# Merge stage of a hybrid-attention step: norm, residual and split of h by runs of 384 columns, gate blocks 0 and 1 by runs between embedding pieces

## The chip, the cores and the metric

One core of one Trainium2 chip. The metric is the device time in microseconds of one execution of the whole program. Several executions are timed and their median is given; one more is recorded by the hardware profiler, and everything said of engines comes from that one.

## The reference, cut to what matters

```python
def merge(oa, za, ob, zb, w_out):
    return jnp.concatenate([oa * jax.nn.silu(za), ob * jax.nn.silu(zb)], axis=-1) @ w_out

def finish(x, mix, p, post_g, w_gate, w_ple, ple_g):
    h = x + rms_norm(mix, post_g)
    return h + jax.nn.sigmoid(h @ w_gate) * rms_norm(p @ w_ple, ple_g)
```

There are 1152 tokens (1024 of a prompt and 8 x 16 of samples) and 1024 features; `w_out` and `w_gate` are 1024 x 1024, `p` has 256 features. Everything ahead of this (the input projection and two attentions) is not touched.

## The kernel before, in words

The program runs in stages, and the last one is the function `merge` (L1508). All data lie feature-major: a block of 128 features is on the 128 partitions, and the 1152 tokens run along the free dimension. A product writes PSUM in three runs of 384 tokens, one bank each (`RUN`, `NCH`); `acc[0]` and `acc[1]` are two sets of three banks, and `small` is two banks more.

A product in near-float32 is three passes (L231): the weight and the data are each split into a high part (`w_hi`, `a_hi`) and a low part (`w_lo`, `a_lo`), and high x high, high x low and low x high are added up. One output block of 128 features over 8 blocks of input features and 3 runs is 72 matmuls of 384 columns. A weight block is loaded by SP's queue (L1575 to L1606) into one of two `w_raw` slots, its high part is made by ScalarE (`high`, L1613), its low part by GpSimd (`low`, L1691).

The stage has these steps:

- Eight blocks of the output projection (`multiply(0)` to `multiply(7)`, L1767). VectorE copies each into `mix` (L1841), ScalarE squares it (L1623), VectorE adds the squares (L1826).
- The embedding p @ w_ple, eight blocks of six plain float32 matmuls (`embed`, L1740; each shows as two records in the trace). Their weights share the two `w_raw` slots with the gate weights. The first two blocks are held in `work` until `mix` has been read.
- Between them: 9 small matmuls sum the squares over the partitions (`statistics(0)`, L1747), VectorE and ScalarE make the reciprocal root, VectorE spreads it over diagonals (L1832), and three matmuls bring it to all partitions (`to_all(0)`, L1756). VectorE copies the three runs into `rms` (L1836).
- h, block by block of 1152 columns: VectorE scales `mix` (L1847); the residual is added into `x` by VectorE for blocks 0 and 2 (L1852) and by GpSimd for the others (L1702); ScalarE moves or takes an embedding block into `mix` (L1653, L1656) and makes the high part of h (L1663); VectorE makes the low part (`low`, L1795), three blocks behind.
- Eight gate blocks h @ w_gate (`multiply(GATE0)` and on, L1777 to L1789). Inside block 1 stands `statistics(1)` and inside block 2 `to_all(1)`, for the norm of the embedding; ScalarE squares all eight embedding blocks (L1623 again) for it. ScalarE takes the sigmoid of each block (L1681), and VectorE finishes the output (L1862, L1869, L1871).

Each engine runs its own list of instructions in the order written, and waits on semaphores. A gate block i of 2 or more writes the banks of block i - 2, and so waits for that block's sigmoid. What GpSimd's queue holds around h is: residual adds 1, 3, 4, 5, the low part of gate weight 0, adds 6 and 7, the low part of gate weight 1.

```python
multiply(GATE0, (h_hi_done, h_lo_done))
multiply(GATE0 + 1, between={5: lambda: statistics(1)})
multiply(GATE0 + 2, between={2: lambda: to_all(1)})
```

Of the kernel before, what the change touches and what calls it, by code (L numbers as in the profile page):

```python
# [243 lines left out]
def run(x, n):  # L244
    return x[:, n * RUN:(n + 1) * RUN]
# [1262 lines left out]
def merge(nc, w_slot, z_sample, xT, pT, w_out, w_gate, w_ple, yT, qo, ident, ones, g_sub, g_post, g_ple):  # L1508
# [5 lines left out]
    PLE0, GATE0, END = NB, 2 * NB, 3 * NB  # L1514
    with ExitStack() as ctx:
# [5 lines left out]
        w_raw, w_hi, w_lo = weight_slots(mk, w_slot)  # L1521
        work = [mk.sb(f"work{s}", [P, TOK]) for s in range(2)]
# [26 lines left out]
        def split_count(j):  # L1549


            return j if j < PLE0 else j - GATE0 + NB

        def loads_of_slot(j):

            here = j // 2 + 1 if j < PLE0 else NB // 2 + 1 + (j >= GATE0) * ((j - GATE0) // 2 + 1)
            return here - (j % 2 == 0 if j < PLE0 or j >= GATE0 else j < PLE0 + NB // 2)

        BY_DVE = (0, 2)

        def wait_h(eng, j):
            if j in BY_DVE:
                eng.wait_ge(h_by_dve, 1 + BY_DVE.index(j))
            else:
                eng.wait_ge(h_by_pool, sum(i not in BY_DVE for i in range(j + 1)))

        def ple_weights(j):

            return w_raw[j // 4][:].rearrange("p (b k) c -> p b k c", k=PKT)[:, j % 4]
# [4 lines left out]
        def _(sp):  # L1574
            sp.dma_start(w_raw[1][:], w_out[1]).then_inc(w_in[1], 16)  # L1575
            for j in range(2, 4):
                if j > 2:
                    sp.wait_ge(w_lo_done, split_count(j - 2))
                sp.dma_start(w_raw[j % 2][:], w_out[j]).then_inc(w_in[j % 2], 16)
# [4 lines left out]
            for j in range(4, NB):  # L1584
                sp.wait_ge(w_lo_done, split_count(j - 2))
                sp.dma_start(w_raw[j % 2][:], w_out[j]).then_inc(w_in[j % 2], 16)
            for r in range(2):
                sp.wait_ge(w_lo_done, split_count(NB - 2 + r))
                sp.dma_start(w_raw[r][:].rearrange("p (b k) c -> p b (k c)", k=PKT),
                             w_ple[4 * r:4 * r + 4].rearrange("b p k c -> p b (k c)")).then_inc(w_in[r], 16)  # L1590
            for r in range(2):
                sp.wait_ge(product, PLE0 + 4 * r + 4)
                sp.dma_start(w_raw[r][:], w_gate[r]).then_inc(w_in[r], 16)
# [5 lines left out]
            for j in range(2, NB):  # L1599
                sp.wait_ge(w_lo_done, split_count(GATE0 + j - 2))  # L1600
                sp.dma_start(w_raw[j % 2][:], w_gate[j]).then_inc(w_in[j % 2], 16)
                if j >= 4:
                    store_y(j - 4)
# [8 lines left out]
        def _(act):  # L1612
            def high(j):  # L1613
                act.wait_ge(w_in[j % 2], 16 * loads_of_slot(j))
                if j >= 2:
                    act.wait_ge(product, j - 1 if j < PLE0 or j >= GATE0 + 2 else NB)
                act.activation(w_hi[j % 2][:], w_raw[j % 2][:], ACT.Copy).then_inc(w_hi_done, 1)
# [21 lines left out]
            for j in range(NB - 2, NB):  # L1639
                act.wait_ge(mix_out, j + 1)  # L1640
                square(j, 0)
            for j in range(2):
                act.wait_ge(product, PLE0 + j + 1)
                act.wait_ge(added, NB - 1 + j)
                act.activation(by_runs(work[j][:]), acc[j][:, :, 0:RUN], ACT.Copy).then_inc(ple_out, 1)
                if j == 0:
                    mix_norm.scalar(act)

            def take_ple(j):
                wait_h(act, j)  # L1650
                if j < 2:
                    act.wait_ge(ple_out, 2)
                    act.activation(mix[:, j, :], work[j][:], ACT.Copy).then_inc(ple_moved, 1)  # L1653
                else:
                    act.wait_ge(product, PLE0 + j + 1)
                    act.activation(by_runs(mix[:, j, :]), acc[j % 2][:, :, 0:RUN], ACT.Copy).then_inc(ple_out, 1)  # L1656

            for j in range(NB):
                if j == 1:
                    take_ple(2)  # L1660
                if j != 2:
                    take_ple(j)
                act.activation(a_hi[:, j, :], x[:, j, :], ACT.Copy).then_inc(h_hi_done, 1)  # L1663
                if j == NB // 2:
                    high(GATE0)
            high(GATE0 + 1)
            act.wait_ge(ple_out, NB)
            act.wait_ge(ple_moved, 2)
            for j in range(NB):
                square(j, NB)  # L1670
            ple_norm.scalar(act)

            for j in range(GATE0, END):
                i = j - GATE0
                act.wait_ge(product, j + 1)
                if i < 2:
                    act.wait_ge(added, 2 * NB)
                else:
                    act.wait_ge(ple_gated, i - 1)
                if j < END - 1:  # L1680
                    act.activation(by_runs(work[j % 2][:]), acc[j % 2][:, :, 0:RUN], ACT.Sigmoid).then_inc(sigmoid, 1)  # L1681
                else:
                    for n in range(NCH):
                        act.wait_ge(product, j + 1 + n)
                        act.activation(run(work[j % 2][:], n), acc[j % 2][:, n, 0:RUN], ACT.Sigmoid).then_inc(sigmoid, 1)
                if j + 2 < END:
                    high(j + 2)

        @block.gpsimd
        def _(pool):  # L1690
            def low(j):  # L1691
                pool.wait_ge(w_hi_done, split_count(j))
                pool.tensor_tensor(w_lo[j % 2][:], w_raw[j % 2][:], w_hi[j % 2][:].bitcast(F32),  # L1693
                                   ALU.subtract).then_inc(w_lo_done, 1)

            for j in range(1, NB):
                low(j)
            pool.wait_ge(x_in, 16 * KT)
            for j in range(1, NB):
                if j not in BY_DVE:  # L1700
                    pool.wait_ge(normed, j + 1)
                    pool.tensor_tensor(x[:, j, :], x[:, j, :], mix[:, j, :], ALU.add).then_inc(h_by_pool, 1)  # L1702
                if j == NB // 2 + 1:
                    low(GATE0)
            for j in range(GATE0 + 1, END):
                low(j)

        @block.tensor
        def _(pe):
            def free_banks(j):  # L1710

                if j >= GATE0 + 2:
                    pe.wait_ge(sigmoid, j - GATE0 - 1)
                elif j >= PLE0 + 2:
                    pe.wait_ge(ple_out, j - PLE0 - 1)
                elif j >= 2:
                    pe.wait_ge(mix_out, j - 1)

            def multiply(j, parts=(), between={}):
                if j > 0:  # L1720
                    pe.wait_ge(w_lo_done, split_count(j))
                free_banks(j)
                for k in range(KT):
# [4 lines left out]
                    for n in range(NCH):  # L1728
                        last = three_passes(pe, acc[j % 2][:, n, 0:RUN], w_hi[j % 2][:, k, :], w_lo[j % 2][:, k, :],
                                            run(a_hi[:, k, :], n), run(a_lo[:, k, :], n),  # L1730
                                            start=(k == 0), stop=(k == KT - 1))
                last.then_inc(product, 1)

            def embed(j):
                i = j - PLE0
                pe.wait_ge(w_in[i // 4], 16 * loads_of_slot(j))
                free_banks(j)
                for k in range(PKT):
                    for n in range(NCH):
                        last = pe.matmul(acc[j % 2][:, n, 0:RUN], ple_weights(i)[:, k, :], run(p_emb[:, k, :], n),  # L1740
                                         start=(k == 0), stop=(k == PKT - 1))
                last.then_inc(product, 1)
# [27 lines left out]
            pe.wait_ge(p_in, 16)  # L1770
            embed(PLE0)
            statistics(0)
            embed(PLE0 + 1)
            to_all(0)
            for j in range(PLE0 + 2, GATE0):
                embed(j)
            multiply(GATE0, (h_hi_done, h_lo_done))  # L1777
            multiply(GATE0 + 1, between={5: lambda: statistics(1)})
            multiply(GATE0 + 2, between={2: lambda: to_all(1)})
            for j in range(GATE0 + 3, END - 1):  # L1780
                multiply(j)
            pe.wait_ge(w_lo_done, split_count(END - 1))
# [9 lines left out]
        def _(dve):  # L1792
# [35 lines left out]
            def spread_norm(norm, which):  # L1828
# [5 lines left out]
                for n in range(NCH):  # L1834
                    dve.wait_ge(spread, NCH * which + n + 1)
# [138 lines left out]
```

## Time and profile before

| | |
|---|---|
| median of 3 runs | 870.44 us (870.25 to 870.54) |
| the profiled execution's own time | 871.64 us |
| its span in the trace | 869.8 us |
| mean granted TensorE clock over the span | 0.973 |
| TensorE matmul busy | 799.1 us, 92% of the span |
| VectorE / ScalarE / GpSimd busy | 412.9 / 332.7 / 192.9 us |
| DMA, mean over the span | 106 GB/s |

Times in rows count from the start of the span. A row of an instruction runs from its start to its acknowledged end, so the next one on the same engine can start some 0.1 us before the row ends; the distance from start to start is what an instruction costs in a full queue. A row that was made to wait inside the engine is longer by that wait. An engine's idle time before a row stands in brackets with what ended it. The merge stage takes the last 265 us.

### The profile page before, as it was taken

What the parts mean: (1) busy time and instruction counts of PE and PEld (TensorE: products, weight loads), DVE (VectorE), ACT (ScalarE), POOL (GpSimd) and SP (SyncE); (2) the same over time, 40 slices, a digit from 0 to 9 for tenths busy, and PEclk for the clock granted to TensorE, in tenths of its full rate; (3) what the DMA queues carried; (4) which work ended last, traced back from release to release, by engine and by line L of the source; (5) the groups of instructions that cost most, each with busy time, mean ns of one, the idle gap of its engine ahead of it and who ended that gap; (6) DMA issues with size and microseconds to landing.
All of it is one profiled execution on the core that took longest, in us unless ns stands there. A gap on an engine that the chain in (4) does not pass through costs nothing. (4 is left out here: it accounts for less than half of the span.)

```text
span 869.8 us, 13090 instructions
## 1 busy us (share of the span) xinstructions
PE 799.1 (92%) x5207; PEld 714.3 (82%) x5207; DVE 412.9 (47%) x947; ACT 332.7 (38%) x679; POOL 192.9 (22%) x165
## 2 busy tenths in 40 slices
PE   5999999999978989697769999997999998899998
PEld 6999999999965657564458999897999984498998
DVE  6743231011039889587572222232613438966553
ACT  7321011100016788597574444345411213452111
POOL 0122122122111000153433333222211203812220
PEclk9999999999999999889899999998899999899999
DMA  8142343212011000390026666761611100102301
GB/s 327 48 179 113 103 157 106 76 49 82 0 29 45 1 1 2 98 382 22 1 98 225 241 237 233 269 226 49 270 75 49 49 0 25 49 25 90 117 33 78
DMA packets 35993, 92.58 MB, mean 106 GB/s; under 512 B 4696, under 2 KB 13912, under 8 KB 33752
## 3 DMA queue, kind: packets, MB, share of 16 engines
q1 hardware_dynamic: 33488, 82.23, 26.7%
q10 hardware_dynamic: 2448, 9.57, 2.9%
q8 instruction: 38, 0.62, 0.3%
q14 instruction: 19, 0.16, 0.1%
HBM read 76.13 MB, written 16.58 MB: 107 GB/s over the span
## 5 line engine op out<-in xcount | busy, mean ns | idle before, releaser
L233 PE MATMUL in_acc<-in_x_hi,w_hi 128*128 128x384 f32 x216 | 74.6, 346 | 9.4 <-DVE in_x_lo L427 8.7
L234 PE MATMUL in_acc<-in_x_lo,w_hi 128*128 128x384 f32 x216 | 74.1, 343 | 0.0
L235 PE MATMUL in_acc<-in_x_hi,w_lo 128*128 128x384 f32 x216 | 74.0, 343 | 0.0
L233 PE MATMUL in_acc<-in_x_hi,in_w_hi 128*128 128x384 f32 x216 | 72.7, 336 | 0.0
L233 PE MATMUL mrg_acc<-mrg_a_hi,w_hi 128*128 128x384 f32 x192 | 67.0, 349 | 6.1 <-issue 3.0
L235 PE MATMUL in_acc<-in_x_hi,in_w_lo 128*128 128x384 f32 x216 | 72.2, 334 | 0.0
L234 PE MATMUL in_acc<-in_x_lo,in_w_hi 128*128 128x384 f32 x216 | 72.2, 334 | 0.0
L234 PE MATMUL mrg_acc<-mrg_a_lo,w_hi 128*128 128x384 f32 x192 | 65.5, 341 | 0.0
L235 PE MATMUL mrg_acc<-mrg_a_hi,w_lo 128*128 128x384 f32 x192 | 65.4, 341 | 0.0
L842 ACT ACTIVATE ahead_ring<-ahead_ring,diff_nmax 128x1024 f32<-128x1024 f32 (+7 forms) x64 | 49.0, 769 | 40.6 <-DVE diff_nmax L799 40.3
L233 PE MATMUL mrg_acc<-mrg_a_hi,mrg_w_hi 128*128 128x384 f32 x192 | 64.2, 334 | 0.0
L235 PE MATMUL mrg_acc<-mrg_a_hi,mrg_w_lo 128*128 128x384 f32 x192 | 64.1, 334 | 0.0
L234 PE MATMUL mrg_acc<-mrg_a_lo,mrg_w_hi 128*128 128x384 f32 x192 | 64.1, 334 | 0.0
L473 DVE SCALAR_TENSOR_TENSOR qo<-in_acc,plane 128x1152 f32<-128x1152 f32 x8 | 10.9, 1358 | 91.4 <-PE in_acc L235 91.4
L741 PE MATMUL diff_score<-plane,qo 64*128 64x512 f32 (+3 forms) x192 | 40.4, 525 | 13.0 <-DVE diff_part L790 5.7
L233 PEld LDWEIGHTS in_acc<-in_x_hi,w_hi 128*128 128x128 f32 x216 | 41.3, 191 | 9.9 <-issue 8.7
L463 DVE TENSOR_TENSOR plane<-in_acc,plane 128x1152 f32<-128x1152 f32 x9 | 12.2, 1357 | 68.2 <-PE in_acc L235 68.2
L323 ACT ACTIVATE in_w_hi<-plane 128x1024 fp32r<-128x1024 f32 x9 | 9.6, 1062 | 90.6 <-PE in_acc L235 76.6
L233 PEld LDWEIGHTS mrg_acc<-mrg_a_hi,w_hi 128*128 128x128 f32 x192 | 37.2, 194 | 7.7 <-issue 5.7
L369 POOL TENSOR_TENSOR w_lo<-w_raw,w_hi 128x1024 fp32r<-128x1024 f32 x8 | 19.1, 2394 | 108.5 <-ACT w_hi L323 108.5
L1841 DVE COPY mrg_mix<-mrg_acc 128x1152 f32<-128x1152 f32 x8 | 10.9, 1358 | 66.0 <-PE mrg_acc L235 66.0
L234 PEld LDWEIGHTS in_acc<-in_x_lo,w_hi 128*128 128x128 f32 x216 | 41.3, 191 | 0.1
(250 smaller groups left out, 1988.5 us busy)
## 6 DMA issues: line engine op xcount, KB each, us to landing
ahead_ring<-kb_cache SPq DMA_DIRECT2D x16, 1024.0 KB, 7.2
ahead_ring<-vb_cache SPq DMA_DIRECT2D x16, 1024.0 KB, 8.3
qo<-xT SPq DMA_DIRECT2D x16, 576.0 KB, 8.1
w_raw<-w_in SPq DMA_DIRECT2D x11, 512.0 KB, 4.0
plane<-w_in SPq DMA_DIRECT2D x9, 512.0 KB, 3.6
h_scratch<-qo SPq DMA_DIRECT2D x8, 576.0 KB, 5.2
plane<-h_scratch SPq DMA_DIRECT2D x8, 576.0 KB, 15.3
yT<-mrg_mix SPq DMA_DIRECT2D x7, 576.0 KB, 3.1
```

Source lines behind the costliest of these rows:

```text
L233: pe.matmul(out, w_hi, x_hi, start=start, stop=False)
L234: pe.matmul(out, w_hi, x_lo, start=False, stop=False)
L235: return pe.matmul(out, w_lo, x_hi, start=False, stop=stop)
L323: act.activation(w_hi[j % 2][:], w_raw[j % 2], ACT.Copy).then_inc(w_hi_done, 1)
L369: pool.tensor_tensor(w_lo[j % 2][:], w_raw[j % 2], w_hi[j % 2][:].bitcast(F32), ALU.subtract).then_inc(w_lo_done, 1)
L463: dve.tensor_tensor(by_runs(to), acc_runs(r), by_runs(rms), ALU.mult).then_inc(evacuated, 1)
L473: dve.scalar_tensor_tensor(out=by_runs(qo[:, k, :]), in0=acc_runs(j % 2), scalar=-SCALE, in1=by_runs(rms), op0=ALU.mult, op1=ALU.mult).the ...
L741: last = pe.matmul(score[m][:, c:c + n], qo[rows, BH + h, t * P:(t + 1) * P], kT[rows, h + 1, c:c + n], start=True, stop=True)
L842: act.activation(prob[i % 4][:, m, 0:n], prob[i % 4][:, m, 0:n], ACT.Exp, scale=-1.0, bias=nmax[i % 2][:, m:m + 1], accum_out=norm[i % 2][ ...
L1841: dve.tensor_copy(by_runs(mix[:, j, :]), acc[j % 2][:, :, 0:RUN]).then_inc(mix_out, 1)
```

## The change

h and the embedding go by pieces. Piece e is block e % 8 of run e // 8: 128 features by 384 tokens; there are 24. All eight pieces of a run are made before those of the next run.

- VectorE scales, adds (blocks 0 and 2) and splits 24 pieces, and copies the scale of a run just ahead of its first piece; GpSimd adds 18 pieces; ScalarE makes 24 high parts.
- The embedding weights get two buffers of their own (`ple_half`), so all eight gate weights go through the two `w_raw` slots right behind the output weights. Gate weights 0 and 1 are split before h: on GpSimd ahead of the residual adds, on ScalarE around the last squares and the first embedding piece.
- The embedding goes by 24 pieces. Pieces 0 to 11 are multiplied before the gates; 0 to 5 and 8 to 11 are held in `work`, piece by piece, and moved later (20 short ScalarE copies), the others are taken from their bank straight into `mix`. Pieces 16 to 23 use two banks in turn, and ScalarE takes them behind the high part of piece 23.
- Gate blocks 0 and 1 are multiplied run by run (`early_gate`): run 0 behind embedding piece 11, run 1 behind piece 15, run 2 behind piece 23.
- `statistics(1)` goes from block 1 into block 2 (before k = 4), `to_all(1)` from block 2 to the start of block 3.
- The sigmoids write `swish` (the place of `p_emb`) instead of `work`. The sigmoid of block 0 stands on ScalarE's queue behind the sixth of the eight squares, that of block 1 behind the eighth, then the weight copy for block 3, then the root of the embedding's norm.

```diff
-    PLE0, GATE0, END = NB, 2 * NB, 3 * NB
+    GATE0, END = NB, 2 * NB
+    PIECES = NCH * NB
+    HELD, BANK_LATE = 12, (1, 2, 4, 5)
+    MOVED = tuple(range(6)) + tuple(range(8, HELD))
+    TAKEN = tuple(range(6)) + tuple(range(8, HELD)) + (6, 7) + tuple(range(HELD, PIECES))
...
+        ple_half = [z_sample, mk.sb("ple_w", [P, SEQ])]
+        swish = [p_emb[:, s, :] for s in range(2)]
...
+        def bank_of(e):
+
+            if e < HELD:
+                return e % (2 * NCH)
+            return BANK_LATE[e - HELD] if e < 2 * NB else (2, 5)[e % 2]
...
         @block.sync
...
+            for q in range(4, 6):
+                load_weight(q)
+            sp.wait_ge(gated, 2)
+            for half in range(2):
+                sp.dma_start(ple_half[half][:].rearrange("p (b c) -> p b c", b=4),
+                             w_ple[4 * half:4 * half + 4].rearrange("b p k c -> p b (k c)")).then_inc(p_in, 16)
+            for q in range(6, GATE0 + 2):
+                load_weight(q)
...
         @block.scalar
...
+            for e in range(6):
+                hold(e)
+                if e == 0:
+                    high(GATE0 + 1)
+                if e == 2:
                     mix_norm.scalar(act)
...
+            for e in range(NB):
+                h_high(e)
+                if e < 6:
+                    move(e)
                 else:
+                    take(e)
+                if NB + e < HELD:
+                    hold(NB + e)
+            for e in range(NB, 2 * NB):
+                h_high(e)
+                if e < HELD:
+                    move(e)
+            for e in range(HELD, 2 * NB):
+                take(e)
+            for e in range(2 * NB, PIECES):
+                h_high(e)
+            for e in range(2 * NB, PIECES):
+                take(e)
...
             for j in range(NB):
                 square(j, NB)
+                if j == 3:
+                    high(GATE0 + 2)
+                if j == 5:
+                    gate(0)
+            gate(1)
+            high(GATE0 + 3)
             ple_norm.scalar(act)
...
         @block.gpsimd
...
+            for q in range(1, GATE0 + 2):
+                low(q)
             pool.wait_ge(x_in, 16 * KT)
...
+            for idx in range(PIECES):
+                if idx % NB not in BY_DVE:
+                    pool.wait_ge(normed, idx + 1)
+                    pool.tensor_tensor(piece(x, idx), piece(x, idx), piece(mix, idx), ALU.add).then_inc(h_by_pool, 1)
...
         @block.tensor
...
+            def embed(e):
+                free_bank(("ple", e), bank_of(e))
                 for k in range(PKT):
...
+            def early_gate(i, n):
+
+                pe.wait_ge(w_lo_done, GATE0 + i)
+                free_bank(("gate", i, n), NCH * i + n)
+                for k in range(KT):
+                    if i == 0:
+                        pe.wait_ge(h_hi_done, NB * n + k + 1)
+                        pe.wait_ge(h_lo_done, NB * n + k + 1)
+                    last = three_passes(pe, bank(NCH * i + n), w_hi[i][:, k, :], w_lo[i][:, k, :],
+                                        run(a_hi[:, k, :], n), run(a_lo[:, k, :], n),
+                                        start=(k == 0), stop=(k == KT - 1))
                 last.then_inc(product, 1)
...
+            for e in range(HELD):
+                embed(e)
+                if e == 2:
+                    statistics(0)
+                if e == 5:
+                    to_all(0)
+            early_gate(0, 0)
+            early_gate(1, 0)
+            for e in range(HELD, 2 * NB):
+                embed(e)
+            early_gate(0, 1)
+            early_gate(1, 1)
+            for e in range(2 * NB, PIECES):
+                embed(e)
+            early_gate(0, 2)
+            early_gate(1, 2)
+            multiply(GATE0 + 2, between={4: lambda: statistics(1)})
+            multiply(GATE0 + 3, between={0: lambda: to_all(1)})
...
         @block.vector
...
+            for idx in range(PIECES):
+                n, j = divmod(idx, NB)
+                if j == 0:
+                    keep(0, n)
+                    dve.wait_ge(rms_done, n + 1)
+                dve.scalar_tensor_tensor(out=piece(mix, idx), in0=piece(mix, idx), scalar=g_post[:, j:j + 1],
+                                         in1=run(rms[:], n), op0=ALU.mult, op1=ALU.mult).then_inc(normed, 1)
                 if j in BY_DVE:
...
+                    dve.tensor_tensor(piece(x, idx), piece(x, idx), piece(mix, idx), ALU.add).then_inc(h_by_dve, 1)
+                if idx >= 3:
+                    h_low(idx - 3)
```

## Rows read from the trace of the kernel before

**Rows 1.** The chain of waits, 650 to 870 us: start, duration, what.
```profile
725.62 1.43 DVE mrg_mix L1847
...
746.20 3.69 POOL qo L1702
...
755.30 2.96 issue
```

**Rows 2.** TensorE's timeline, 705 to 800 us: start, duration, line, operation, idle before.
```profile
724.83 7.90 PE L1740 MATMUL mrg_acc<-mrg_p_emb,w_raw 128*128 128x384 f32 x24
736.16 9.67 PE L1740 MATMUL mrg_acc<-mrg_p_emb,mrg_w_raw 128*128 128x384 f32 x24 [3.43 <-ACT mrg_mix L1656]
...
758.25 0.66 PE L233 MATMUL mrg_acc<-mrg_a_hi,w_hi 128*128 128x384 f32 x1 [2.96 <-issue]
...
780.02 2.06 PE L1747 MATMUL mrg_small<-consts,mrg_total 128*128 128x1 f32 x18
...
788.42 0.45 PE L233 MATMUL mrg_acc<-mrg_a_hi,w_hi 128*128 128x384 f32 x1 [1.54 <-POOL w_lo L1693]
...
791.65 2.43 PE L1756 MATMUL mrg_small<-mrg_total,consts 128*128 128x384 f32 x6
```

**Rows 3.** Windows: length, PE, PEld, DVE, ACT, POOL busy, granted clock, DMA.
```profile
612.30:712.24 99.94, 99.94 (x570) 99.11 (x569) 33.01 (x20) 18.89 (x17) 17.03 (x7) 0.99 0.27 96
...
732.80:741.00 8.20, 4.84 (x10) 2.72 (x11) 8.20 (x4) 5.31 (x6) 4.51 (x2) 0.79 0.17 64
...
758.20:772.20 14.00, 13.95 (x72) 13.98 (x73) 11.01 (x8) 8.82 (x9) 6.47 (x2) 0.89 0.22 78
...
786.90:800.80 13.90, 12.29 (x64) 11.17 (x65) 7.66 (x8) 2.08 (x2) 3.85 (x2) 1.00 0.20 69
```

**Rows 4.** VectorE's timeline, 705 to 800 us.
```profile
720.09 1.85 DVE L1832 TENSOR_SCALAR mrg_total<-consts,mrg_mix_norm_rstd 128x128 f32<-128x128 f32 x9
723.40 1.20 DVE L1836 COPY mrg_rms<-mrg_small 128x384 f32<-128x384 f32 x2 [1.46 <-PE mrg_small L1756]
...
741.08 1.35 DVE L1795 TENSOR_TENSOR mrg_a_lo<-qo,mrg_a_hi 128x1152 fp32r<-128x1152 f32 x1
...
746.04 1.35 DVE L1795 TENSOR_TENSOR mrg_a_lo<-qo,mrg_a_hi 128x1152 fp32r<-128x1152 f32 x1
...
758.13 7.62 DVE L1795 TENSOR_TENSOR mrg_a_lo<-qo,mrg_a_hi 128x1152 fp32r<-128x1152 f32 x4
...
797.56 1.36 DVE L1871 TENSOR_TENSOR mrg_mix<-mrg_mix,qo 128x1152 f32<-128x1152 f32 x1
798.83 1.41 DVE L1862 SCALAR_TENSOR_TENSOR mrg_mix<-mrg_mix,gain,mrg_rms 128x1152 f32<-128x1152 f32 x1
```

**Rows 5.** GpSimd's timeline, 520 to 605 and 600 to 800 us.
```profile
533.89 2.39 POOL L1223 TENSOR_TENSOR smp_w_lo<-w_raw,smp_w_hi 128x1024 fp32r<-128x1024 f32 x1 [10.36 <-ACT smp_w_hi L1444]
536.25 1.99 POOL L1230 TENSOR_TENSOR qo<-qo,smp_swish 128x384 f32<-128x384 f32 x2
...
749.84 3.47 POOL L1693 TENSOR_TENSOR w_lo<-w_raw,w_hi 128x1024 fp32r<-128x1024 f32 x1
```

**Rows 6.** GpSimd's groups by form: count, busy us, mean ns of one, idle before.
```profile
L1230 POOL TENSOR_TENSOR qo<-qo,smp_swish 128x384 f32<-128x384 f32 x16 | 15.9, 1011 | 0.0
```

**Rows 7.** ScalarE's timeline, 560 to 604 and 705 to 800 us.
```profile
589.59 0.49 ACT L1457 ACTIVATE smp_swish<-smp_acc 128x384 f32<-128x384 f32 x1
589.98 0.45 ACT L1481 ACTIVATE qo<-smp_mixed 64x64 f32<-64x64 f32 x2
...
765.06 2.21 ACT L1623 ACTIVATE mrg_work<-mrg_mix 128x1152 f32<-128x1152 f32 x2
...
782.55 1.28 ACT L1681 ACT_TABLE_LOAD   x1
783.85 1.13 ACT L1681 ACTIVATE mrg_work<-mrg_acc 128x1152 f32<-128x1152 f32 x1
784.88 1.05 ACT L1617 ACTIVATE w_hi<-w_raw 128x1024 fp32r<-128x1024 f32 x1
```

More of the change, by code:

```diff
@@ L1599, in _ @@
             for j in range(2, NB):
[L1600 to L1601 removed]
+                load_weight(GATE0 + j)
                 if j >= 4:
@@ L1658, in _ @@
[L1658 to L1668, printed above, removed]
+            act.wait_ge(mix_out, NB - 1)
+            square(NB - 2, 0)
+            high(GATE0)
@@ new lines, in _, with hold, move @@
+            act.wait_ge(mix_out, NB)
+            square(NB - 1, 0)
+            def hold(e):
+                act.wait_ge(product, after(("ple", e)))
+                if e < NB:
+                    act.wait_ge(added, NB - 1 + e // NCH)
+                else:
+                    act.wait_ge(ple_moved, moved(e - NB))
+                act.activation(held(e), bank(bank_of(e)), ACT.Copy).then_inc(ple_out, 1)
+            def move(e):
+                act.wait_ge(ple_out, taken(e))
+                act.activation(piece(mix, e), held(e), ACT.Copy).then_inc(ple_moved, 1)
@@ L1669, in _ @@
+            act.wait_ge(ple_out, PIECES)
+            act.wait_ge(ple_moved, len(MOVED))
             for j in range(NB):
                 square(j, NB)
-            ple_norm.scalar(act)
[L1673 to L1687, printed above, removed]
+                if j == 3:
+                    high(GATE0 + 2)
+                if j == 5:
+                    gate(0)
@@ L1719, in multiply, with free_banks, free_bank @@
[L1719 to L1722, printed above, removed]
+            def free_banks(q):
+                if q >= GATE0 + 2:
+                    pe.wait_ge(sigmoid, q - GATE0 - 1)
+                elif q >= 2:
+                    pe.wait_ge(mix_out, q - 1)
+            def free_bank(what, b):
+                last = last_in_bank(b, order.index(what))
+                if last is None:
+                    pe.wait_ge(mix_out, NB - 1 + b // NCH)
+                else:
+                    pe.wait_ge(ple_out, taken(last))
@@ L1866, in _ @@
                     part = (lambda a: a) if j < NB - 1 else (lambda a: run(a, n))
-                    y, gate = part(mix[:, j, :]), part(work[j % 2][:])
+                    y, gate = part(mix[:, j, :]), part(swish[j % 2])
                     dve.wait_ge(sigmoid, j + 1 + n)
```

195 lines of the change are left out of this document (93 added, 102 removed).

## Prediction

> **What bounds the kernel now.** I read the chain of waits first, from the end of the output projection to the gate blocks. At 725.62 it is on VectorE's norm of the mix, goes on through GpSimd's residual add, one ScalarE copy and the embedding, and reaches the gate blocks after 2.96 us in which TensorE waited for nothing that the profile names [rows 1]. The reader should see that TensorE does not bind this stretch, the one where h is made: the engines that make h do.
>
> Second, TensorE's timeline: the matmuls of that stretch are the same before and after the change, so the time moves only with TensorE's gaps, with its clock, and with what is put between two products. The gaps are 3.43 us at 736.16, 2.96 at 758.25 and 1.54 at 788.42 [rows 2]. Third, the windows: in the two stretches that hold the long gaps the granted clock averaged 0.79 over 8.2 us and 0.89 over 14 us, which cost 0.21 x 8.2 = 1.7 and 0.11 x 14 = 1.5 us. After the 1.54 gap it stayed 1.00 [rows 3]. So gaps of about 3 us are followed by some time at the lower level (1.2 GHz), the short one was not.
>
> Fourth, VectorE's and GpSimd's rows, for what makes h slow. A round of one block is norm, residual and low part; the low parts start at 741.08 and 746.04, a round of 4.96 us [rows 4]. Alone, a 1152-column VectorE instruction takes 1.27 from start to start (797.56 to 798.83 [rows 4]). GpSimd's 1024-column subtraction alone takes 2.36 (533.89 to 536.25), and two 384-column ones take 1.99, so 0.98 from start to start, as a single row is 1.01 [rows 5, 6]; on that slope 1152 columns are 0.98 + 768 x 2.16 ns = 2.63. 2 x 1.27 + 2.63 = 5.17 against 4.96: in this stretch the two engines work in turn, never side by side, and 0.21 us of fixed cost per round hides behind the other's turn. **The h stage is bound by the sum of VectorE and GpSimd**, from 725.62 to the last low part at 765.75.
>
> **The change, part by part.**
>
> *Start of h.* The norm of piece 0 needs only run 0's scale: the first copies start at 723.40, two in 1.20, so it can start at 724.0 instead of 725.62 [rows 1, 4]. Gain 1.6. The six pieces of embedding in front of it cost what two blocks cost now, and the statistics and the spreading stand at the same places between them.
>
> *The weight splits moved out.* GpSimd's split of gate block 0 (a row of 3.47 at 749.84, part of it waiting [rows 5]) and that of block 1 move ahead of h, beside the last output block and the embedding. Their loads, and the two embedding loads, are issued earlier on SP's queue, into buffers that are free by then (the embedding's own are not shared with a gate weight any more). TensorE hides all of it; bare of that cover it would be one row of 3.47. The second split may hold back the small norm instructions by a few tenths; I take nothing.
>
> *h in pieces.* VectorE goes from 18 instructions of 1152 columns to 54 of 384, GpSimd from 6 to 18. A 384-column VectorE instruction: between 128 columns (nine in 1.85, 0.206 each) and 1152 (1.27) on a line, 0.47 [rows 4]. A round with GpSimd is 2 x 0.47 + 0.98 = 1.92 with no fixed cost hidden; a third of today's round is 1.65, all of it hidden. I take 1.92 - 0.21 = 1.71, say 1.72, because the hidden part per round should not depend on the length. Pieces 0 and 2 of a run are three VectorE instructions, 1.41. A run: 6 x 1.72 + 2 x 1.41 + 0.5 for its copy = 13.64. Three runs, 40.9: the last low part at 764.9, GpSimd's last add three VectorE instructions earlier at 763.5, ScalarE's high part of piece 23 done at 764.1 (a 384-column ScalarE instruction: 0.39 from 589.59 to 589.98 [rows 7]). So 72 short instructions take about as long as 24 long ones with a split among them.
>
> *Gate blocks 0 and 1 early.* 48 of the 72 matmuls of each now run inside the h stage, and TensorE has room for them: a matmul of a split product is 0.173 (the 576 of the output projection in 99.94 [rows 3]), so 96 x 0.173 = 16.6 us of products and twelve embedding pieces, 15.8, in 40. But the last third does not start when h is done. ScalarE's queue has the copies of embedding pieces 16 to 23 behind the high part of piece 23, those pieces have two banks, and the products of the third run stand behind them on TensorE. So from 764.1: one copy, 0.4; six embedding pieces at 7.90 / 6 = 1.32 [rows 2], 8.0; half of one clock loss, 0.85 (bounds 0 and 1.7: the gap before them is 2 to 3 us, between the gap that cost nothing and those that cost 1.5 and 1.7); the last copy with hand-overs, 0.7. That gives 774.1. The products of the third run, 2 x 24 x 0.173 = 8.3, end near 782 and are not the bound.
>
> *From there to gate block 2.* It waits for the sigmoid of block 0, because it writes the same banks; on ScalarE's queue that sigmoid has six squares and a weight copy in front. Two squares 2.2, one add 1.3, two squares 2.2, the weight copy 1.05, two squares 2.2, the table load 1.28, the sigmoid 1.13: 11.4 [rows 4, 7]. **Gate block 2 starts at 785.5**, against 788.42: a gain of 2.9. The weight's low part is ready near 784, so the sigmoid is what is late next; behind TensorE's wait stand all other gate blocks.
>
> At this switch of tables the load starts at 782.55, takes 1.28, and the sigmoid starts at 783.85 [rows 7]: 1.3 in all. The Trainium skill (ScalarE: Activation LUTs, "What ACT_TABLE_LOAD costs") gives a switch as the same load of 1283 ns and a drain of about 1380 ns behind it. By that rule the start would be at 786.9 and the sum below 1.4 larger; the trace does not agree, it shows no room for the drain.
>
> *After that start.* The statistics of the embedding stood in block 1, ahead of it; now they stand in block 2: 2.06 more behind it [rows 2]. The spreading, 2.43, stays behind it. And the gap in front of the block grows from 1.54 to 785.5 - 782 = 3.5 us, like those of 3.43 and 2.96 that cost 1.7 and 1.5 at the lower clock; I take 1.6 (bounds 0, as after 1.54, and 1.7). The two further table loads lie beside TensorE's block 2 and 3; without that cover they are 1.28 each. From block 4 on nothing changes.
>
> **Sum:** -2.9 + 2.06 + 1.6 = +0.8 us; with the few tenths of the small norm instructions, +0.9. The profiled execution took 871.64 for a span of 869.8; it would take 872.5. It stands 1.2 above the median of the runs, 870.44, to which I add the same: **871.3 us**.
>
> **Rivals.**
>
> *The pieces are dear (slower).* If the short instructions hide nothing, a round is 1.92 and 18 of them add 3.6: +4.5, 874.9. It happens at the VectorE and GpSimd queues between 724 and 765; above a round of 1.77 it decides (0.9 + 18 x 0.05 = 1.8). For it: each short instruction now has a wait in front, and the rows with hidden cost are long ones. Against it: the measured 0.21.
>
> *The clock stays up and the pieces are cheap (faster).* Rounds of 1.65 take off 1.3, no loss in front of the six embedding pieces 0.85, and the full clock in block 2 another 1.6: -2.8, 867.6. For it: the low level followed gaps of 3 us but not 1.54, so its point lies somewhere between. Against it: without the full clock in block 2 it does not decide, and cheap rounds and that clock together are only just enough (0.9 - 1.3 - 1.6 = -2.0).
>
> *The early products give all they could (faster).* If the copies of pieces 16 to 23 were done by 764.1 + 8 x 0.41 = 767.4, block 2 would start at 778.8: -9.6 + 2.06 + 1.6 = -6, 864.4. The order written on ScalarE's queue excludes it, unless banks free earlier than I read. That the change did not do what it says would look the same as no change, and I see no such thing in the diff.
>
> *The switch of tables costs its load twice (slower).* Another 1.28 us on ScalarE in front of the first sigmoid, which TensorE waits for: +2.2, 872.6. The two rows back to back speak against it. It is the mechanism of the Trainium skill's rule named above, priced by the row of the load.
>
> **How the numbers follow.** A measurement of this kernel can tell 0.2%, 1.7 us, from no change. Forecast, the gain in h given back behind it: 0.45. Dear pieces 0.34, the dear switch 0.03: slower 0.37. Cheap pieces with full clock 0.16, early products in full 0.02: faster 0.18. The forecast's own range is 868.7 to 872.1. The range for 8 in 10 takes in most of both neighbours: from 868.0 (one clock loss gone and cheap rounds) to 874.6 (rounds of 1.9).
>
> **What would show it.** In the profile after: the norm of piece 0 near 724.0; rounds of 1.7 on GpSimd's rows; high part of piece 23 near 764; then six embedding pieces one behind another on TensorE while VectorE idles; the first sigmoid with a table load in front, and block 2 at 785.5 after a gap of 3 to 4 us with a granted clock under 1 behind it; two table loads more. Wrong would be: rounds of 1.9, block 2 before 784 or after 788.5, or VectorE and GpSimd running side by side on short instructions.

## The result, and the profile after

The changed kernel takes **873.81 us** (median of 8 executions, 871.82 to 874.73); the kernel before, beside it, 870.61 (870.25 to 871.71). The ratio is 1.003 with a 95% interval of 1.0017 to 1.0043: slower by about 3 us. That is inside the range and on the side that was given 0.37; the forecast of 871.3 is 2.5 too low.

The profiled execution took 874.73 us for a span of 872.9, 0.9 above its median. I count from the first embedding piece to the end of the last matmul, which leaves out what differs ahead of the change. Of the kernel before, TensorE's timeline, first and last row of that stretch:

```profile
712.24 4.03 PE L1740 MATMUL mrg_acc<-mrg_p_emb,w_raw 128*128 128x384 f32 x12
...
865.52 0.34 PE L235 MATMUL mrg_acc<-mrg_a_hi,mrg_w_lo 128*128 128x384 f32 x1
```

That is 865.86 - 712.24 = 153.62 us. TensorE's timeline of the changed kernel:

```profile
712.54 4.03 PE L1809 MATMUL mrg_acc<-mrg_p_emb,strip_then_z 128*128 128x384 f32 x12
...
736.51 0.41 PE L233 MATMUL mrg_acc<-mrg_a_hi,w_hi 128*128 128x384 f32 x1 [3.41 <-issue]
...
760.28 2.74 PE L1809 MATMUL mrg_acc<-mrg_p_emb,strip_then_z 128*128 128x384 f32 x8
...
765.23 4.49 PE L1809 MATMUL mrg_acc<-mrg_p_emb,strip_then_z 128*128 128x384 f32 x8 [2.21 <-ACT mrg_mix L1699]
...
787.04 0.66 PE L233 MATMUL mrg_acc<-mrg_a_hi,w_hi 128*128 128x384 f32 x1 [3.83 <-ACT mrg_p_emb L1735]
...
795.86 2.06 PE L1829 MATMUL mrg_small<-consts,mrg_total 128*128 128x1 f32 x18
...
868.63 0.34 PE L235 MATMUL mrg_acc<-mrg_a_hi,mrg_w_lo 128*128 128x384 f32 x1
```

868.97 - 712.54 = 156.43 us: 2.81 longer. Gate block 2 starts 74.50 us after the stretch began, before 76.18 [rows 2]: **1.68 sooner**. But from there to the end it is 81.93 against 77.44: **4.49 longer**. The statistics now stand in that part, 1.92 from their start to the next product (795.86 to 797.78). The rest, 2.57, is the clock: 17 products from 787.04 on take 5.5 us instead of 2.9. The windows of the changed kernel show it (columns as in [rows 3]):

```profile
766.00:776.00 10.00, 10.00 (x32) 6.24 (x31) 0.00 (x0) 3.51 (x7) 0.00 (x0) 0.87 0.00 0
...
783.00:787.00 4.00, 0.21 (x2) 0.00 (x0) 3.66 (x3) 3.97 (x5) 2.41 (x1) 0.83 0.07 7
787.00:793.00 6.00, 5.96 (x20) 5.99 (x21) 3.80 (x3) 5.37 (x5) 1.67 (x1) 0.54 0.22 85
793.00:800.00 7.00, 7.00 (x49) 7.00 (x48) 1.63 (x9) 0.21 (x1) 0.70 (x1) 1.00 0.00 1
```

The granted clock falls to its lower level (1.2 GHz) inside the gap in front of block 2 and stays there for about 5.5 us of the block, where it was 1.00 before [rows 3]. The embedding pieces 18 and 19 ran mostly at the lower level too: 4.49 us for the eight records that took 2.74 at 760.28.

The h stage itself is on VectorE's timeline of the changed kernel:

```profile
723.77 0.56 DVE L1928 COPY mrg_rms<-mrg_small 128x384 f32<-128x384 f32 x1 [1.53 <-PE mrg_small L1838]
724.37 0.62 DVE L1948 SCALAR_TENSOR_TENSOR mrg_mix<-mrg_mix,gain,mrg_rms 128x384 f32<-128x384 f32 x1
...
757.59 0.55 DVE L1932 TENSOR_TENSOR mrg_a_lo<-qo,mrg_a_hi 128x384 fp32r<-128x384 f32 x1
...
759.35 0.55 DVE L1932 TENSOR_TENSOR mrg_a_lo<-qo,mrg_a_hi 128x384 fp32r<-128x384 f32 x1
...
762.85 2.75 DVE L1932 TENSOR_TENSOR mrg_a_lo<-qo,mrg_a_hi 128x384 fp32r<-128x384 f32 x4
```

A round is 1.76 us from low part to low part, and the last low part ends at 765.60. Before, a round of three times the columns took 4.96 [rows 4]; a third of that is 1.65. The short instructions cost 0.1 us a round more than that third. GpSimd's timeline has the matching adds, and the split that comes late next:

```profile
761.26 1.25 POOL L1770 TENSOR_TENSOR qo<-qo,mrg_mix 128x384 f32<-128x384 f32 x1 [0.50 <-DVE mrg_mix L1948]
763.00 1.24 POOL L1770 TENSOR_TENSOR qo<-qo,mrg_mix 128x384 f32<-128x384 f32 x1 [0.50 <-DVE mrg_mix L1948]
782.43 2.98 POOL L1761 TENSOR_TENSOR w_lo<-w_raw,w_hi 128x1024 fp32r<-128x1024 f32 x1 [18.19 <-ACT w_hi L1656]
```

What block 2 waits for stands on ScalarE's timeline, of which the chain of waits from 764.27 to 787.04 takes nearly every row:

```profile
764.27 0.52 ACT L1703 ACTIVATE mrg_a_hi<-qo 128x384 fp32r<-128x384 f32 x1 [1.21 <-POOL qo L1770]
764.70 0.85 ACT L1699 ACTIVATE mrg_mix<-mrg_acc 128x384 f32<-128x384 f32 x2
...
774.91 0.49 ACT L1699 ACTIVATE mrg_mix<-mrg_acc 128x384 f32<-128x384 f32 x1 [0.80 <-PE mrg_acc L1809]
775.44 2.22 ACT L1662 ACTIVATE mrg_work<-mrg_mix 128x1152 f32<-128x1152 f32 x2
779.18 2.23 ACT L1662 ACTIVATE mrg_work<-mrg_mix 128x1152 f32<-128x1152 f32 x2 [1.52 <-DVE mrg_total L1914]
781.31 1.04 ACT L1656 ACTIVATE w_hi<-w_raw 128x1024 fp32r<-128x1024 f32 x1
782.25 2.20 ACT L1662 ACTIVATE mrg_work<-mrg_mix 128x1152 f32<-128x1152 f32 x2
784.47 1.28 ACT L1735 ACT_TABLE_LOAD   x1
785.77 1.13 ACT L1735 ACTIVATE mrg_p_emb<-mrg_acc 128x1152 f32<-128x1152 f32 x1
```

The reader should see one queue: the last high part, the copies that wait for six embedding pieces, six squares and a weight copy, then the sigmoid.

### The profile page after: what moved, and what is told of

It reads as the page before. It is cut to its first block and busy times, and to the rows that moved or that the text cites. A ratio compares the mean times of both kernels' runs of the same rounds, so it can differ in the third digit from the quotient of the medians.

```text
span 872.9 us, 13190 instructions
## 1 busy us (share of the span) xinstructions
PE 800.4 (92%) x5207; PEld 715.8 (82%) x5207; DVE 414.9 (48%) x983; ACT 341.9 (39%) x721; POOL 192.8 (22%) x177
## 5 line engine op out<-in xcount | busy, mean ns | idle before, releaser
L233 PE MATMUL in_acc<-in_x_hi,w_hi 128*128 128x384 f32 x216 | 74.5, 345 | 10.7 <-DVE in_x_lo L427 10.0
L233 PEld LDWEIGHTS mrg_acc<-mrg_a_hi,w_hi 128*128 128x128 f32 x192 | 38.1, 198 | 11.4 <-issue 10.7
```

The costliest lines, as they stand in the source:

```text
L233: pe.matmul(out, w_hi, x_hi, start=start, stop=False)
```

## The experiments

My theory: the h stage is not dearer; what is won in it is lost to two places in ScalarE's queue, which keep TensorE waiting, to the clock behind those waits, and to the statistics, which now stand behind the start of block 2. The rivals: the short pieces are dear, the early products are in the way, or the 0.3% is no difference at all.

The experiments ran in four groups, on four chips, each group beside the kernel before (medians 871.3, 871.04 and 871.25 us in the three that give a ratio). Single executions spread wider there: the kernel before took 868.1 to 874.1 us in 23 of them. The trace shows that the spread arises ahead of the change: the first embedding piece starts anywhere from 709.0 to 715.4 us, while the stretch behind it repeats to 0.01 us in the three kernels that were profiled twice. So beside each median stands the stretch, from first embedding piece to end of last matmul, and its two parts, all in us. Each stretch is that of one profile.

| kernel | median | ratio to before (95%) | stretch | start of block 2 | from there to the end |
|---|---|---|---|---|---|
| before | 870.61 | | 153.62 | 76.18 | 77.44 |
| changed | 873.81 | 1.003 (1.0017 to 1.0043) | 156.43 | 74.50 | 81.93 |
| changed, again | 873.69 | 1.002 (1.0005 to 1.0036) | 156.42 | 74.49 | 81.93 |
| copies of pieces 16, 17 earlier | 868.89 | 0.998 (0.9965 to 0.9994) | 152.94 | 71.09 | 81.85 |
| sigmoid and weight copy earlier | 867.80 | 0.9968 (0.9953 to 0.9982) | 151.56 | 70.50 | 81.06 |
| sigmoid alone earlier | 871.26 | 0.9996 (0.9978 to 1.0014) | 154.01 | 72.97 | 81.04 |
| gap filled with dummies | 871.1 | 1.0 (0.9984 to 1.0016) | 153.97 | 74.55 | 79.42 |
| gate runs behind all embedding | 885.64 | 1.0178 (1.0156 to 1.02) | 168.87 | 89.41 | 79.46 |
| both moves | 865.43 | 0.9925 (0.9907 to 0.9943) | 148.19 | 67.12 | 81.07 |
| both, sums spread out | 864.27 | 0.9916 (0.9899 to 0.9933) | 146.88 | 67.11 | 79.77 |
| both, sums one k later | 864.48 | 0.9921 (0.99 to 0.9943) | 146.45 | 67.11 | 79.34 |

**The changed kernel again.** No edit.

> The changed kernel once more, unaltered, beside the edited ones and in more rounds, because the kernel before spread from 867.9 to 873.8 us in the earlier group of runs. My theory (the change costs 3 us: block 2 starts 1.7 us sooner, but has 2.06 us of statistics and 2.7 us of lower clock behind it): 873 to 874 us, ratio to the kernel before 1.002 to 1.005. Rival (the 0.3% were the disturbance of those executions): ratio 0.999 to 1.001.

Measured: 873.69 us, ratio 1.002 (1.0005 to 1.0036), the stretch 156.42. The loss is real and sits behind the start of block 2.

**Copies of pieces 16 and 17 ahead of the last high part.**

```diff
             for e in range(2 * NB, PIECES):
                 h_high(e)
+                if e == PIECES - 2:
+                    take(2 * NB)
+                    take(2 * NB + 1)
-            for e in range(2 * NB, PIECES):
+            for e in range(2 * NB + 2, PIECES):
                 take(e)
```

> Edit: ScalarE takes embedding pieces 16 and 17 behind the high part of piece 22, not of piece 23. Theory (the gain in h is handed back by the order of ScalarE's queue behind it): TensorE goes on with piece 18 near 763.5 instead of 765.23, the gap of 2.21 us in front of it shrinks to some 0.6 and no lower clock follows it, so the last take ends near 772.3 instead of 775.4 and gate block 2 starts near 784 instead of 787.04; 873.8 becomes 870 to 871. Rival (h itself is the bound, the short pieces are dear): h is not touched, so no change, 873.8.

TensorE's timeline of that kernel:

```profile
763.65 2.85 PE L1812 MATMUL mrg_acc<-mrg_p_emb,strip_then_z 128*128 128x384 f32 x8 [0.42 <-ACT mrg_mix L1699]
...
783.82 0.66 PE L233 MATMUL mrg_acc<-mrg_a_hi,w_hi 128*128 128x384 f32 x1 [3.84 <-ACT mrg_p_emb L1738]
```

The gap in front of piece 18 falls from 2.21 to 0.42, the eight records take 2.85 instead of 4.49, and block 2 starts 3.4 us sooner (71.09 against 74.50). Nothing behind it changes: the gap of 3.84 and its lower clock are still there. So two copies of 0.4 us in the wrong place of ScalarE's queue cost 3.4 us, half of it wait and half clock.

**Weight copy and sigmoid of block 0 ahead of the third square.** The statistics go behind k = 6, because the squares are done later.

```diff
             for j in range(NB):
                 square(j, NB)
-                if j == 3:
+                if j == 1:
                     high(GATE0 + 2)
-                if j == 5:
                     gate(0)
...
-            multiply(GATE0 + 2, between={4: lambda: statistics(1)})
+            multiply(GATE0 + 2, between={6: lambda: statistics(1)})
```

> Edit: on ScalarE's queue the weight copy for block 2 and the sigmoid of block 0 stand behind the second square instead of the fourth and sixth; the statistics go from before k = 4 to before k = 6 of block 2. Theory: the products of blocks 0 and 1 end at 783.0 as now, the sigmoid ends near 782.4, so block 2 starts near 783.1 with a gap under 1 us in front of it (now 3.83) and at the full clock: 4.0 for the gap and 2.7 for the clock, 873.8 becomes 867 to 868. Rival (the weight's low part on GpSimd sets the start, not the sigmoid): the start moves no further than 785.5, and 873.8 becomes 872 or so.

ScalarE's timeline of that kernel, and one of its windows:

```profile
778.13 1.06 ACT L1656 ACTIVATE w_hi<-w_raw 128x1024 fp32r<-128x1024 f32 x1 [1.48 <-PE mrg_acc L235]
779.21 1.28 ACT L1735 ACT_TABLE_LOAD   x1
780.50 1.14 ACT L1735 ACTIVATE mrg_p_emb<-mrg_acc 128x1152 f32<-128x1152 f32 x1
```

```profile
794.00:798.00 4.00, 4.00 (x17) 4.00 (x16) 2.59 (x13) 0.06 (x1) 0.06 (x1) 0.61 0.01 2
```

Block 2 follows the third-run products without a gap, 4.0 us sooner, and its products run at full clock. What I had not seen coming is the window: behind the statistics the clock falls to 0.61 over 4 us, so most of the clock's share is given back there.

**Sigmoid alone.** Only `gate(0)` moves, to right behind `high(GATE0 + 2)`, which stays at j == 3; the statistics stay at k = 4.

> Only the sigmoid of block 0 moves: behind the weight copy of block 2, ahead of the fifth and sixth square; the weight copy stays behind the fourth. Theory: the sigmoid is done near 784.9, and GpSimd's low part of the weight, which ended at 785.41 in the changed kernel, is late next: block 2 near 785.5, -1.5 us, with a gap of 2.4 us and the lower clock behind it as before: about 872.3 us. Rival (the sigmoid is the only thing that block 2 waits for, and a shorter gap keeps the clock up): -2.1 for the start and -2.7 for the clock, 869 us.

TensorE's timeline of that kernel:

```profile
782.14 0.44 PE L233 MATMUL mrg_acc<-mrg_a_hi,w_hi 128*128 128x384 f32 x1 [2.25 <-POOL w_lo L1760]
```

The start is 1.53 sooner, as expected, and the releaser is now GpSimd's split of the weight: the sigmoid was not the only late thing, the weight copy in front of that split was the next. The gap of 2.25 still cost the lower clock, though less of it: the part behind the start is 81.04 against 81.93.

**The gap filled.** 22 products of no use, into a bank that nobody reads then, between the third-run products and block 2.

```diff
             early_gate(1, 2)
+            for _ in range(22):
+                pe.matmul(small[:, 1, 0:RUN], a_hi[:, 0, 0:P], run(a_hi[:, 0, :], 0), start=True, stop=True)
```

> Edit: 22 matmuls whose result nobody reads stand between the last product of block 1 and block 2, about 3.8 us of work in the gap. Theory: block 2 starts at 787.0 as now, and the rest of its first 5.3 us goes at the higher clock instead of the lower one: 2.7 us less, 873.8 becomes 871.1. Rival (the lower clock has another cause than the gap in front of it, or it is taken later instead): the same time or, with the extra matmuls in the way, up to 0.5 us more.

TensorE's timeline and a window of that kernel:

```profile
780.77 3.98 PE L1870 MATMUL mrg_small<-mrg_a_hi 128*128 128x384 f32 x22
```

```profile
785.00:791.00 6.00, 6.00 (x36) 6.00 (x36) 3.60 (x3) 5.11 (x5) 1.87 (x1) 1.00 0.17 69
```

Block 2 starts where it did (74.55), at clock 1.00, and the part behind it falls from 81.93 to 79.42: 2.51 us by the clock alone. What is left, 79.42 - 77.44 = 1.98, is the statistics.

**Gate runs behind all embedding pieces.** This takes the early products away and keeps the pieces.

```diff
-        order = ([("ple", e) for e in range(HELD)] + [("gate", 0, 0), ("gate", 1, 0)]
-                 + [("ple", e) for e in range(HELD, 2 * NB)] + [("gate", 0, 1), ("gate", 1, 1)]
-                 + [("ple", e) for e in range(2 * NB, PIECES)] + [("gate", 0, 2), ("gate", 1, 2)])
+        order = [("ple", e) for e in range(PIECES)] + [("gate", i, n) for n in range(NCH) for i in range(2)]
```

(TensorE's calls of `embed` and `early_gate` follow the same order.)

> Edit: h and the embedding by pieces as in the change, but all six run products of gate blocks 0 and 1 stand behind embedding piece 23 on TensorE. Theory (the early products are worth something, and their gain is hidden behind the sigmoid): the four products that moved add 4 x 24 x 0.173 = 16.6 us behind 774.4, so block 1 ends near 799.5 with no gap behind it; block 2 starts 12.5 us later than 787.04 but at the full clock, 873.8 becomes 883 to 884, slower than the kernel before. Rival (early products are hidden anyway): no change.

ScalarE's timeline of that kernel, then TensorE's:

```profile
793.61 1.06 ACT L1654 ACTIVATE w_hi<-w_raw 128x1024 fp32r<-128x1024 f32 x1 [14.37 <-PE mrg_acc L235]
```

```profile
799.37 0.41 PE L233 MATMUL mrg_acc<-mrg_a_hi,w_hi 128*128 128x384 f32 x1 [1.69 <-ACT mrg_p_emb L1733]
```

The start of block 2 is 14.9 us later than in the changed kernel, so without the early products the kernel loses that much; they are not in the way. It is later than I expected, because the copy of block 2's weight waits for the last product of gate block 0, now the fifth of six. The 1.69 us gap in front of the block is followed by no lower clock:

```profile
799.00:805.00 6.00, 5.63 (x32) 5.66 (x33) 3.55 (x3) 5.59 (x6) 1.62 (x1) 1.00 0.19 78
```

**Both moves together.** The edits of the copies and of the sigmoid with the weight copy, statistics behind k = 6.

> The copies of pieces 16 and 17 ahead of the high part of piece 23, and the weight copy and sigmoid of block 0 behind the second square, together; statistics behind the sixth k of block 2. Theory (two queue positions on ScalarE set the start of block 2, and the gap in front of it sets the clock): last embedding copy near 771.7, third-run products 771.2 to 779.8, sigmoid done near 779, so block 2 at 779.8 without a gap. Against the changed kernel -7.2 for the start, -2.7 for the clock in block 2, +1.6 for the lower clock behind the statistics, as it was with the sigmoid moved alone: -8.3, about 865.5 us, faster than both kernels. Rival (the two gains overlap, because after the earlier copies the products of the third run end just as late or GpSimd's low part of the weight takes over): no better than the sigmoid moved alone, 867.8 us.

Measured: 865.43 us, the stretch 148.19, which is 8.24 less than changed; block 2 starts at 67.12 without a gap, 7.4 sooner. The gains add. Weight loads of TensorE and a window of that kernel:

```profile
788.72 2.08 PEld L1831 LDWEIGHTS mrg_small<-consts,mrg_total 128*128 128x128 f32 x18 [0.21 <-DVE mrg_total L1919]
```

```profile
792.00:796.00 4.00, 4.00 (x15) 3.87 (x14) 2.02 (x10) 0.00 (x0) 0.00 (x0) 0.57 0.00 0
```

TensorE comes to the sums 0.21 us too early, by its weight loads, as it does with the sigmoid and weight copy moved alone, and 1.3 us behind them the clock falls again.

**The sums spread out.** One or two columns at a time among the products of k = 6 and 7, the spreading behind k = 0 of block 3. This edit and those that follow are against the kernel with both moves.

```diff
+            COLUMNS = {(6, 0): (0, 1), (6, 1): (2, 3), (6, 2): (4, 5), (7, 0): (6,), (7, 1): (7,), (7, 2): (8,)}
...
+                        if (k, n) in between:
+                            between[k, n]()
...
-            multiply(GATE0 + 3, between={0: lambda: to_all(1)})
+            multiply(GATE0 + 3, between={1: lambda: to_all(1)})
```

> As the version with both moves, but the nine one-column sums of the statistics stand one or two at a time among the products of the seventh and eighth k of block 2, and the spreading of the result behind the first k of block 3. Theory A (a stretch of 2.2 us of one-column matmuls counts for the clock like a gap): the lower clock behind the statistics goes, 1.6 us less than with both moves together, about 864 us. Theory B (the lower clock there came from something else, such as the waits of the spreading): it stays, the same time as with both moves within 0.5 us. If the later spreading delays VectorE's finish of block 0 so far that block 4 waits for its sigmoid, the time is longer by that wait, up to 1 us.

Measured: 864.27 us, the stretch 146.88, 1.31 less, and the clock 1.00 from 759 to 800. That is theory A's time. A row of the weight loads of this kernel says one thing more:

```profile
788.33 0.52 PEld L1835 LDWEIGHTS mrg_small<-consts,mrg_total 128*128 128x128 f32 x4 [0.21 <-DVE mrg_total L1924]
```

TensorE comes to the first of the sums just as early as with both moves, 0.21 us, and the clock stays up. So the early arrival alone does not lower it. Whether the block of sums alone does, this run cannot say.

**The sums one k later, in one block.**

```diff
-            multiply(GATE0 + 2, between={6: lambda: statistics(1)})
-            multiply(GATE0 + 3, between={0: lambda: to_all(1)})
+            multiply(GATE0 + 2, between={7: lambda: statistics(1)})
+            multiply(GATE0 + 3, between={1: lambda: to_all(1)})
```

> As the version with both moves, but the nine one-column sums stand in one block behind the seventh k of block 2 instead of the sixth, and the spreading behind the first k of block 3. In the version with both moves TensorE reached the sums 0.2 us before VectorE's last add was done (idle of the weight loads, 0.21), and the clock fell 1.3 us behind them; in the kernel before and in the changed kernel the same sums, reached late, left the clock at 1.00. Theory B' (the small wait together with the sums makes the clock fall, the sums alone do not): no wait and no lower clock behind the sums; from the first embedding piece to the last matmul 146.6 to 147.0 us, as with the sums spread out (146.88), against 148.19 with both moves. Theory A (a block of one-column matmuls in a stretch that runs without gaps makes it fall): lower clock behind the sums again, 148.0 to 148.5 us.

TensorE's timeline and a window of that kernel:

```profile
793.43 2.06 PE L1831 MATMUL mrg_small<-consts,mrg_total 128*128 128x1 f32 x18
```

```profile
796.00:798.00 2.00, 2.00 (x13) 2.00 (x12) 1.86 (x10) 0.00 (x0) 0.00 (x0) 1.00 0.01 4
```

No wait, the clock at 1.00 behind the sums, which end near 795.5, and the stretch 146.45. Theory A falls: the same block of sums, reached late, leaves the clock up. This stretch is the shortest here. The ratio of 0.9921 is 0.8% under the kernel before, and cannot be told from the 0.9916 of the version with the sums spread out.

**Both once more, and the wait covered.** Three single executions: both moves again, the version before this one again, and both moves with two dummy products in front of the sums at k = 6:

```diff
             def statistics(which):
+                if which == 1:
+                    for _ in range(2):
+                        pe.matmul(small[:, 1, 0:RUN], a_hi[:, 0, 0:P], run(a_hi[:, 0, :], 0), start=True, stop=True)
                 pe.wait_ge(added, NB * (which + 1))
```

> The version with both moves once more, for one further profile. In its first profile the clock fell 1.3 us behind the nine sums of the embedding's norm, which TensorE reached 0.2 us too early. But the nine sums of the mix's norm, reached 0.3 us too early in every profile, left the clock at 1.00. If the early arrival at this place is the cause, the clock falls again, 148.0 to 148.4 us from the first embedding piece to the last matmul. If it was chance, it stays, 146.4 to 146.9 us.

> The version with the sums behind the seventh k once more, for one further profile. If the late arrival at the sums keeps the clock up, 1.00 behind them again and 146.3 to 146.6 us from the first embedding piece to the last matmul. If it was chance, a stretch of lower clock behind the sums may show, 147.8 to 148.3 us.

> The version with both moves, the sums behind the sixth k as there, but two dummy products of 384 columns, 0.35 us, are issued ahead of them: TensorE reaches the sums when VectorE's last add is done, so the wait is gone and the place is the same. If the wait is the cause, the clock stays at 1.00 behind the sums and the stretch from the first embedding piece to the last matmul is 146.7 to 147.0 us (148.19 less 1.6 of lower clock, plus 0.2). If the place or chance is the cause, the lower clock can show again, 148.2 to 148.6 us.

The single times are 862.94, 861.67 and 864.59 us, beside 870.44 of the kernel before. Both moves again: the stretch 148.20, and the clock at 0.50 from 790 to 792, behind sums that end near 787.5. The later sums again: 146.46, and the clock at 1.00 in the same window, behind sums that end near 789.5. The two windows, in that order:

```profile
790.00:792.00 2.00, 2.00 (x8) 2.00 (x7) 0.86 (x5) 0.00 (x0) 0.00 (x0) 0.50 0.00 0
```

```profile
790.00:792.00 2.00, 2.00 (x13) 2.00 (x12) 1.86 (x10) 0.00 (x0) 0.00 (x0) 1.00 0.02 4
```

With the wait covered, a window of that kernel early in it, and another one behind its sums, which end near 790.9:

```profile
717.00:721.00 4.00, 4.00 (x8) 2.14 (x7) 2.62 (x14) 0.70 (x2) 0.11 (x1) 0.57 0.40 131
...
792.00:794.00 2.00, 2.00 (x14) 2.00 (x13) 1.93 (x11) 0.00 (x0) 0.00 (x0) 1.00 0.01 4
```

Behind the sums at k = 6 the clock stays at 1.00. The stretch is nevertheless 148.49, not 147, because in this execution the clock fell at another place, behind the sums of the mix's norm at 714.67, which TensorE reaches 0.30 us too early in every kernel here. From embedding piece 16 on it is 99.06 us (759.76 to 858.82), against 100.44 with both moves (759.93 to 860.37): 1.38 less. So at k = 6 it takes both: the early arrival and, right behind it, the nine sums in one block. Without the wait (sums later, or the wait covered) the clock stays up, and with the wait but the sums spread out it stays up too. The covered wait and the spread sums rest on one profile each.

## Why the prediction was right or wrong

*Right: what bounds h, and that its pieces are not dear.* The norm of piece 0 was forecast at 724.0 and starts at 724.37, in a stretch that itself begins 0.30 later. A round of 1.72 was forecast, 1.76 measured; the rival's 1.92 is refuted, and the 1.77 above which it would decide was just not reached. The last low part ended at 765.30 on the scale of before, forecast 764.9. This step gave away 0.4 us.

*Right: where the gain ends.* The early products did not bring the start of block 2 forward by what they are worth, because the copies of pieces 16 to 23 stand behind the last high part. Moving two of them (3.4 us) shows it.

*Wrong in size: the clock loss in the six embedding pieces.* I took half a loss, 0.85; it was a whole one, 1.75 (4.49 against 2.74). From the end of the last high part, 764.4, to the first square, 775.14 (both on the scale of before), it took 10.7 instead of 10.0.

*Right: the chain of six squares, weight copy, table load and sigmoid*, 11.4 forecast and 11.6 measured (775.44 to 787.04). The sigmoid starts at 785.77 right behind a load of 1.28 that began at 784.47, so the rival of the dear table switch is refuted. The drain of about 1380 ns that the Trainium skill gives (ScalarE: Activation LUTs, "What ACT_TABLE_LOAD costs") is not in this trace either, neither behind the load nor in front of it, where the square ends at 784.45 (782.25 and 2.20); nor is it behind the load in the kernel with the sigmoid moved (779.21 and 1.28, sigmoid at 780.50).

With the 0.3 of the high part these make block 2 start at 786.74 instead of 785.5: a gain of 1.7 instead of 2.9.

*Wrong in size: the clock in block 2.* Forecast 1.6, bounds 0 and 1.7; measured 2.57, outside the bounds. I had bounded it by the gaps of before, 2.96 and 3.43, though my own sum made the new gap 3.5, and it became 3.83. The statistics cost 1.92 of the forecast 2.06.

The sum by these sizes: -1.68 + 1.92 + 2.57 = +2.81, which is what the trace shows. The three terms and their signs were the right ones; the two losses of the clock were taken too small, by 0.9 and 1.0 us. The rival of the clock that stays up was the wrong way round: the clock went down twice in full, and that made the kernel slower.

That the time lies within the range all the same is in part luck. The upper end, 874.6, was set for rounds of 1.9, which did not come; nothing in it allowed for a larger loss of the clock. And +3.2 us lies nearer to the +4.5 of the rival with the dear pieces than to the forecast of +0.9, so the time alone would have spoken for the wrong mechanism; the rounds in the trace and the moved copies and sigmoid tell the two apart.

## What to carry to other kernels

When products are split to run early, look at what the next in-order queue holds between their last input and the first wait behind them: here two ScalarE copies and four squares in the wrong place held TensorE back by 7.4 us, and moving them made the same change 0.8% faster than the kernel before instead of 0.3% slower. Price a new gap in front of TensorE as the gap and the clock behind it; here gaps of 1.5 and 1.7 us cost no clock, those from 2.2 us up cost 1.5 us of it or more, and none cost half of that. Where executions spread, measure the stretch between two rows of the trace that enclose the change.

## What the runs showed of the hardware that was not expected

The clock's loss behind a gap was not in proportion to it. Gaps of 1.54 (before [rows 2, 3]) and 1.69 us (gate runs behind all embedding pieces) were followed by a clock of 1.00. Behind gaps of 2.20 and 2.21 in front of embedding pieces eight records took 4.5 us instead of 2.74, and in front of block 2 a gap of 2.25 cost some 1.6 us of clock (81.04 less 79.42, the part without a gap). A gap of 3.43 cost no more, 1.8 (9.67 against 7.90 for 24 records [rows 2]), but one of 3.83 cost 2.5 (81.93 less 79.42). Behind gaps of 0.42 to 0.47 the eight records took 2.85, and in the profile with the sums spread out the clock was 1.00 there.

A block of nine one-column sums, 2.1 us, left the clock up in all the kernels that reached it without a wait. In all three profiles in which TensorE came to the embedding's sums 0.21 us early and they stood in one block, the clock fell 1.3 us behind them. TensorE waits longer in front of the mix's sums, in the kernel before and in all the others:

```profile
716.57 2.08 PEld L1747 LDWEIGHTS mrg_small<-consts,mrg_total 128*128 128x128 f32 x18 [0.92 <-DVE mrg_total L1826]
```

By its weight loads that is 0.92 us (0.30 by its matmuls), against the 0.21 of the embedding's sums, and still the clock fell there in one profile of fourteen only. So the length of the wait alone does not decide. Why the one place is hit each time and the other rarely stays open; no run here tells it.
